# Even attention: another order of scores, transposes, copies and exponentials, and the head sums behind the first projection pair

## The chip, the core and the metric

One Trainium2 chip, one of its cores. The metric is the device time of one execution of the whole kernel in microseconds; the median of several runs counts. The engines are TensorE (PE; its weight loads are listed as PEld), VectorE (DVE), ScalarE (ACT), GpSimd (POOL) and SyncE (SP), which issues most transfers.

## The reference, cut to what matters

The kernel computes two blocks of two layers each on 512 tokens of 1024 features (and 256 context tokens). The change concerns the attention of the first layer of the first block. It has 8 heads with two maps each of width 32; the two softmaxes are subtracted with a factor `lam`, applied to values of width 64, and each head is normalised afterwards. Queries are 512 tokens that look at 768 keys (context and tokens), and 256 context queries that look at the context alone.

```python
def diff_attend(q, k, v, lam):
    s = jnp.einsum('bqhmd,bkhmd->bhmqk', q, k).astype(jnp.float32) * (A_QK ** -0.5)
    p = jax.nn.softmax(s, axis=-1)
    a = p[:, :, 0] - lam * p[:, :, 1]
    return jnp.einsum('bhqk,bkhd->bqhd', a, v.astype(jnp.float32))

def diff_attention_post(o, subln, lam_init):
    B, N = o.shape[:2]
    return (rms_norm(o, subln) * (1.0 - lam_init)).reshape(B, N, BRANCH_W)
```

Its output, gated, is multiplied with `w_out[0]` (1024 x 1024), normalised and added to the stream. Before this stage come modulation, input norm and input projection, and after it the odd layer and the second block; all of these are unchanged.

## The kernel before, in words

All five engines run one program each and meet through semaphores. Each engine works strictly in the order in which its program is written.

The even attention runs over 48 units `EVEN_UNITS` = (hp, t, a): head pair hp (4), query tile t of 128 rows (6), head a of the pair (2). Tiles t < 4 are token queries with 768 keys (large units), tiles 4 and 5 context queries with 256 keys (small units). Units 12 to 15, for instance, are the first large ones of the second head pair.

- `even_scores(u)` on TensorE (L556) makes both maps of unit u, in three terms (high times high, high times low, low times high), into banks 0 to 2 or 3 to 5. It waits until the exponentials of unit u-2 have read these banks (`ea["exp"]`).
- VectorE takes the maximum (`even_max`, L1613). ScalarE makes the two exponentials (`even_exp`, L1074), one for each map, with row sums. VectorE divides and mixes the two maps (L1627, L1628, L1631), which signals `probs`. It runs over the units in order: mix u, then maximum of u+2, and at some units other work: low parts of the next head pair (`even_lo`, L1567, behind (t, a) = (2, 0)), the gate of the previous one (`gated_head`, L1616), the split of `eob` (L1422, L1423, behind (4, 1)), and at u = 20 and 37 the split of a weight panel of the output projection (`split_at`, L1403 and L1404).
- `even_transposes(u, kts, n)` (L482) transposes the mixed probabilities, key tiles 0 to 3 into bank 6 and then 4 and 5 into the same bank; between them ScalarE must have copied the bank (`even_copy`, L941, into `ept`; semaphores `transposed` and `copied`, counted by `moved`). Small units have only key tiles 4 and 5.
- `even_pv(p, half)` (L587) multiplies the copies of a pair of units (both heads of one tile) with the values, half of the key tiles at a time, into bank 7. `even_out` on ScalarE copies bank 7 out.
- ScalarE in a step u: both exponentials of u+1, then both copies of u, then at some units `even_hi` (high parts of the next head pair), `even_out` and `even_square`.

On TensorE a step u is: scores of u+2, wait for `probs` of u, transposes 0 to 3 of u, one half of the values of an earlier pair, transposes 4 and 5 of u.

Behind the attention come `head_sums(t)` (L622: sums of squares of each head, two columns a product), the output projection in eight steps `out0_pair(i)` (L329 to L331, L385 to L387), the first two with parts of the other branch that are ready early, and `head_spread(t)` (L632). VectorE makes variances from the four head sums, ScalarE the root, VectorE the inverse. SyncE loads weight panels 1 and 2 of this projection once the scores of units 23 and 47 are done.

Of the kernel before, what the change touches and what calls it, by code (L numbers as in the profile page):

```python
# [28 lines left out]
ACT = mybir.ActivationFunctionType  # L29
# [5 lines left out]
P = 128  # L35
D = 1024
KT = D // P
TX, TC = 512, 256
TA = TX + TC
# [49 lines left out]
def build_kernel(nc, dram, out):  # L89
    with ExitStack() as ctx:  # L90
# [42 lines left out]
        stat = sb("stat", [P, 96])  # L133
# [190 lines left out]
        def _(pe):  # L324
# [194 lines left out]
            for e in range(2, 16):  # L519
# [7 lines left out]
                if e in MOD1_AFTER:  # L527
                    m = MOD1_AFTER.index(e)
# [74 lines left out]
            even_scores(1)  # L603
            mod_columns(1, 11)
            pe.wait_ge(mod_ready, 6)
            for u, (hp, t, a) in enumerate(EVEN_UNITS):
                if u + 2 < len(EVEN_UNITS):
                    even_scores(u + 2)
                pe.wait_ge(ea["probs"], u + 1)
                if t < 4:  # L610
                    even_transposes(u, range(4), moved[u])
                if u >= 2:
                    even_pv(u // 2 - 1, u % 2)
                even_transposes(u, range(4, 6), moved[u] + (t < 4))
            even_pv(len(EVEN_UNITS) // 2 - 1, 0)
            even_pv(len(EVEN_UNITS) // 2 - 1, 1)

            def head_sums(t):

# [31 lines left out]
                    if i == KT - 1:  # L651
                        last.then_inc(panel_done, 1)

            for t in range(3):
                head_sums(t)
            out0_pair(0)
            head_sums(3)
            out0_pair(1)
            pe.wait_ge(ea["out"], 8)
            for t in range(4):  # L660
# [66 lines left out]
            n = 0  # L727
# [197 lines left out]
        def _(act):  # L925
# [14 lines left out]
            def copy(o, in_, func=ACT.Identity, **kw):  # L940
                return act.activation(o, in_, func, **kw)  # L941
# [120 lines left out]
            act.wait_ge(ea["lam"], 1)  # L1062
            tell(copy(lam4[:, 0:2], lam4[:, 0:2], ACT.Exp), ea["lam_exp"], 1)

            def even_exp(u):
                t, b = EVEN_UNITS[u][1], 3 * (u % 2)
                act.wait_ge(ea["negmax"], u + 1)
                if u >= 3:
                    act.wait_ge(ea["transposed"], moved[u - 2])
                flat = ps[:, b:b + 3, :].rearrange("p b n -> p (b n)")  # L1070
                for m in range(2):
                    n = TA if t < 4 else TC
                    at = m * (TA if t < 4 else 512)
                    act.activation(prob[u % 3][:, m, 0:n], flat[:, at:at + n], ACT.Exp,  # L1074
                                   bias=stat[:, 2 * (u % 4) + m:2 * (u % 4) + m + 1],
                                   accum_out=stat[:, 8 + u % 4:9 + u % 4] if m else stat[:, 32 + u:33 + u])\
                        .then_inc(ea["exp"], 1)

            def even_copy(u):
                if u >= 4:  # L1080
                    act.wait_ge(ea["pv"], u // 2 - 1)
                for i, kts in enumerate(((0, 4), (4, 6))[2 - EVEN_MOVES[u]:]):
                    act.wait_ge(ea["transposed"], moved[u] + i + 1)
                    copy(ept[u % 4][:, kts[0]:kts[1], :], ps[:, 6, 0:(kts[1] - kts[0]) * P]
                         .rearrange("p (k n) -> p k n", n=P)).then_inc(ea["copied"], 1)

            def even_square(hp):
                copy(esq[:, hp, :], eot[:, hp, :], ACT.Square).then_inc(ea["sq"], 1)
# [3 lines left out]
                cols = (slice(0, TX), slice(TX, TA))[part]  # L1092
                tell(copy(eot[:, hp, cols], ps[:, 7, 0:(TX, TC)[part]]), ea["out"], 2 * hp + part + 1)

            even_exp(0)
            for u, (hp, t, a) in enumerate(EVEN_UNITS):
                if u + 1 < len(EVEN_UNITS):
                    even_exp(u + 1)
                even_copy(u)
                if (t, a) == (1, 0) and hp < 3:  # L1100
                    even_hi(hp + 1)
                if (t, a) == (0, 1) and hp:
                    even_out(hp - 1, 1)
                    even_square(hp - 1)
                elif (t, a) == (4, 1):
                    even_out(hp, 0)
            act.preload_act_table(ACT.Sqrt)
            even_out(3, 1)
            even_square(3)
# [273 lines left out]
        def _(dve):  # L1383
# [239 lines left out]
            for u, (hp, t, a) in enumerate(EVEN_UNITS):  # L1623
                n = TA if t < 4 else TC
                i = u % 4
                dve.wait_ge(ea["exp"], 2 * u + 2)
                step(dve.reciprocal(stat[:, 12 + i:13 + i], stat[:, 8 + i:9 + i]))  # L1627
                step(dve.scalar_tensor_tensor(out=stat[:, 16 + i:17 + i], in0=stat[:, 32 + u:33 + u], scalar=lam4[:, 3:4],  # L1628
                                              in1=stat[:, 12 + i:13 + i], op0=ALU.mult, op1=ALU.mult))
                p = prob[u % 3]  # L1630
                dve.scalar_tensor_tensor(out=p[:, 0, 0:n], in0=p[:, 1, 0:n], scalar=stat[:, 16 + i:17 + i],  # L1631
                                         in1=p[:, 0, 0:n], op0=ALU.mult, op1=ALU.add).then_inc(ea["probs"], 1)
                if u + 2 < len(EVEN_UNITS):
                    even_max(u + 2)
                if (t, a) == (2, 0) and hp < 3:
                    even_lo(hp + 1)
                if (t, a) == (2, 1) and hp:
                    dve.wait_ge(ea["out"], 2 * hp)
                    gated_head(hp - 1)
                if (t, a) == (4, 1):  # L1640
                    split_tensor(h1hi, h1lo, np.s_[:, 4 + hp, :], eob[:, hp, :], ea["mixed"], hp + 1)
                if u in (20, 37):
                    split_at(FIRST["out0"] + (u == 37))
# [450 lines left out]
```

## Time and profile before

| | us |
|---|---|
| median of 3 runs | 2546.95 |
| lowest and highest run | 2537.63, 2559.36 |
| the profiled execution | 2544.75 |
| its span | 2543.0 |
| TensorE busy in the span | 2344.8 (92%) |
| VectorE busy | 1411.4 (56%) |
| ScalarE busy | 588.8 (23%) |

The profile comes from one execution. Times in it count from the start of the span. A row of instructions gives line, engine and operation, output and inputs, the count, busy time and mean duration, and the idle time of the engine before them with what released it. Matmuls overlap in the pipeline, so the distance from start to start tells more than a matmul's own duration. PEclk is the clock granted to TensorE as a share of 2.4 GHz.

### The profile page before, as it was taken

To read this page: it belongs to the slowest core of one execution; us is meant where nothing else is said; L and a number is where in the kernel's file an instruction comes from. 1 tells how busy PE (TensorE), PEld (TensorE's weight loads), DVE (VectorE), ACT (ScalarE), POOL (GpSimd) and SP (SyncE) were. 2 spreads that over 40 slices of the span, in tenths; PEclk is the share of its full clock that TensorE was granted. 3 is DMA by queue.
4 is the path that set the end of the run, shared out by engine and by line. 5 is a ranking of instruction groups with operands and counts; after the bars stand their busy time and mean duration, and the time that the engine had idled before them with its cause. 6 is when DMAs were issued, how large, how long until landed. Compare 5 with 4: busy or idle time off the path is not lost.

```text
span 2543.0 us, 28907 instructions
## 1 busy us (share of the span) xinstructions
PE 2344.8 (92%) x12276; PEld 1918.4 (75%) x12276; DVE 1411.4 (56%) x1673; ACT 588.8 (23%) x1138; POOL 88.1 (3%) x57
## 2 busy tenths in 40 slices
PE   6999898999999978987799999999999999999997
PEld 5787786667878744675478888879988787888886
DVE  2232336774463068564957776354478734787633
ACT  2111005552230246125622111011110001211100
POOL 0000000000000122021100000000000000000000
PEclk9899997568899999997899999999999999999998
DMA  8022120000121201110012232222222122232222
GB/s 335 18 100 99 71 112 34 18 1 17 67 83 51 84 24 48 59 67 17 34 67 83 100 100 79 93 94 83 87 80 83 67 99 100 83 100 93 85 92 79
DMA packets 30704, 196.03 MB, mean 77 GB/s; under 512 B 3440, under 2 KB 3696, under 8 KB 12528
## 3 DMA queue, kind: packets, MB, share of 16 engines
q1 hardware_dynamic: 29136, 188.03, 21.0%
q10 hardware_dynamic: 1440, 6.16, 0.7%
q8 instruction: 97, 1.59, 0.3%
q14 instruction: 31, 0.25, 0.0%
HBM read 192.08 MB, written 2.10 MB: 76 GB/s over the span
## 4 chain that ended last, share of the span: by engine, by line
PE 85%; DVE 11%; ACT 2%; issue 1%; POOL 1%; DMA 1%; SPq 0%; DVEq 0%; ACTq 0%; POOLq 0%
PE ps L329 20%; PE ps L330 20%; PE ps L331 20%; PE ps L385 3%; PE ps L386 3%; PE ps L387 3%; PE ps L482 3%; PE ps L556 2%; PE ps L438 2%; PE ps L587 1%; PE ps L764 1%; PE ps L741 1%; PE ps L422 1%; PE ps L917 1%; PE ps L463 1%
## 5 line engine op out<-in xcount | busy, mean ns | idle before, releaser
L1403 DVE CAST whi<-raw 128x2048 fp32r<-128x2048 f32 (+2 forms) x162 | 183.8, 1135 | 484.8 <-DMA raw<-in_ffn_out 117.5
L329 PE MATMUL ps<-h2hi,whi 128*128 128x512 f32 x1040 | 409.3, 394 | 18.3 <-DVE h2lo L1500 12.2
L330 PE MATMUL ps<-h2lo,whi 128*128 128x512 f32 x1040 | 406.9, 391 | 0.0
L331 PE MATMUL ps<-h2hi,wlo 128*128 128x512 f32 x1040 | 406.6, 391 | 0.0
L1404 DVE TENSOR_TENSOR wlo<-raw,whi 128x2048 fp32r<-128x2048 f32 (+2 forms) x162 | 341.6, 2109 | 5.6
L329 PE MATMUL ps<-h1hi,whi 128*128 128x512 f32 (+1 forms) x768 | 276.4, 360 | 16.4 <-DVE h1lo L1445 8.3
L330 PE MATMUL ps<-h1lo,whi 128*128 128x512 f32 (+1 forms) x768 | 271.4, 353 | 0.0
L331 PE MATMUL ps<-h1hi,wlo 128*128 128x512 f32 (+1 forms) x768 | 269.1, 350 | 0.0
L329 PEld LDWEIGHTS ps<-h2hi,whi 128*128 128x128 f32 x1040 | 196.7, 189 | 60.9 <-issue 13.8
L331 PEld LDWEIGHTS ps<-h2hi,wlo 128*128 128x128 f32 x1040 | 196.6, 189 | 41.3
L330 PEld LDWEIGHTS ps<-h2lo,whi 128*128 128x128 f32 x1040 | 196.8, 189 | 40.3
L329 PE MATMUL ps<-mhi,whi 128*128 128x512 f32 x544 | 213.0, 392 | 6.6 <-DVE mlo L1423 3.9
L330 PE MATMUL ps<-mlo,whi 128*128 128x512 f32 x544 | 212.6, 391 | 0.0
L331 PE MATMUL ps<-mhi,wlo 128*128 128x512 f32 x544 | 212.5, 391 | 0.0
L329 PEld LDWEIGHTS ps<-h1hi,whi 128*128 128x128 f32 x768 | 148.9, 194 | 43.6 <-issue 17.7
L330 PEld LDWEIGHTS ps<-h1lo,whi 128*128 128x128 f32 x768 | 148.4, 193 | 20.1 <-issue 1.8
L331 PEld LDWEIGHTS ps<-h1hi,wlo 128*128 128x128 f32 x768 | 147.8, 192 | 20.3
L941 ACT ACTIVATE temp<-ps 128x512 f32<-128x512 f32 (+1 forms) x48 | 25.4, 564 | 439.9 <-PE ps L331 433.8
L385 PE MATMUL ps<-whi,h2hi 128*128 128x256 f32 x416 | 119.8, 288 | 8.0 <-DVE h2lo L1500 4.4
L329 PEld LDWEIGHTS ps<-mhi,whi 128*128 128x128 f32 x544 | 102.8, 189 | 29.2 <-issue 4.3
L386 PE MATMUL ps<-wlo,h2hi 128*128 128x256 f32 x416 | 119.4, 287 | 0.0
L387 PE MATMUL ps<-whi,h2lo 128*128 128x256 f32 x416 | 119.3, 287 | 0.0
(247 smaller groups left out, 3573.5 us busy)
## 6 DMA issues: line engine op xcount, KB each, us to landing
raw<-in_ffn_in SPq DMA_DIRECT2D x44, 1024.0 KB, 4.9
raw<-in_ffn_out SPq DMA_DIRECT2D x32, 704.0 KB, 4.1
raw<-in_even SPq DMA_DIRECT2D x16, 1024.0 KB, 7.0
mod_w<-in_mod SPq DMA_DIRECT2D x6, 2048.0 KB, 25.7
mraw<-in_mod SPq DMA_DIRECT2D x12, 1024.0 KB, 4.9
raw<-in_odd SPq DMA_DIRECT2D x12, 1024.0 KB, 4.9
raw<-in_sgu_v SPq DMA_DIRECT2D x12, 1024.0 KB, 4.8
raw<-in_sgu_u SPq DMA_DIRECT2D x12, 1024.0 KB, 4.8
```

The lines of the kernel that those rows point to most:

```text
L329: pe.matmul(o, r(lhi), r(rhi), start=first, stop=False, **kw)
L330: pe.matmul(o, r(lhi), r(rlo), start=False, stop=False, **kw)
L331: return pe.matmul(o, r(llo), r(rhi), start=False, stop=last, **kw)
L385: pe.matmul(o, lhi, rhi, start=first, stop=False, **kw)
L386: pe.matmul(o, lhi, rlo, start=False, stop=False, **kw)
L387: return pe.matmul(o, llo, rhi, start=False, stop=last, **kw)
L422: last = pe.matmul(mod_bank(layer, k)[32 * g:32 * g + 32, :], cs[:, kt, :], panel[:, kt * 256:(kt + 1) * 256], start=half == 0, stop=half ...
L438: done = pe.matmul(ps[:, 6, 48 + t:49 + t], tile[:, t * P:(t + 1) * P], ones[:, 0:1], start=first and t == tiles[0], stop=last, skip_group ...
L482: return pe.transpose(o, in_, ident)
L556: return pe.matmul(o, r(q), r(k), start=i == 0, stop=i == 2)
L1403: step(dve.tensor_copy(whi[:, slot, 0:width].bitcast(F32R), raw[:, slot, 0:width]))
L1404: tell(dve.tensor_tensor(wlo[:, slot, 0:width].bitcast(F32R), raw[:, slot, 0:width], whi[:, slot, 0:width], ALU.subtract), split_done, n + 1)
```

## The change

On TensorE a step u becomes: scores of u+2, transposes 4 and 5 of u-1, one half of the values of an earlier pair (half a pair later than before), wait for `probs` of u, transposes 0 to 3 of u. On ScalarE a step u becomes: first copy of u-1, first exponential of u+1, second copy of u-1, second exponential of u+1; `even_hi`, `even_out` and `even_square` move one unit later. On VectorE `gated_head` moves one unit later. Transposes still use the transpose mode of TensorE. Behind the attention the first projection pair comes before the four head sums, where it came behind three of them.

```diff
--- before.py
+++ after.py
@@ -603,17 +603,21 @@
             even_scores(1)
             mod_columns(1, 11)
             pe.wait_ge(mod_ready, 6)
+            last_unit = len(EVEN_UNITS) - 1
             for u, (hp, t, a) in enumerate(EVEN_UNITS):
-                if u + 2 < len(EVEN_UNITS):
+                if u < last_unit - 1:
                     even_scores(u + 2)
+                if u:
+                    even_transposes(u - 1, range(4, 6), moved[u] - 1)
+                if u >= 3:
+                    even_pv((u - 3) // 2, (u - 3) % 2)
                 pe.wait_ge(ea["probs"], u + 1)
                 if t < 4:
                     even_transposes(u, range(4), moved[u])
-                if u >= 2:
-                    even_pv(u // 2 - 1, u % 2)
-                even_transposes(u, range(4, 6), moved[u] + (t < 4))
-            even_pv(len(EVEN_UNITS) // 2 - 1, 0)
-            even_pv(len(EVEN_UNITS) // 2 - 1, 1)
+            even_pv((last_unit - 2) // 2, 1)
+            even_transposes(last_unit, range(4, 6), moved[last_unit + 1] - 1)
+            even_pv(last_unit // 2, 0)
+            even_pv(last_unit // 2, 1)
 
             def head_sums(t):
 
@@ -651,10 +655,9 @@
                     if i == KT - 1:
                         last.then_inc(panel_done, 1)
 
-            for t in range(3):
+            out0_pair(0)
+            for t in range(4):
                 head_sums(t)
-            out0_pair(0)
-            head_sums(3)
             out0_pair(1)
             pe.wait_ge(ea["out"], 8)
             for t in range(4):
@@ -1062,27 +1065,27 @@
             act.wait_ge(ea["lam"], 1)
             tell(copy(lam4[:, 0:2], lam4[:, 0:2], ACT.Exp), ea["lam_exp"], 1)
 
-            def even_exp(u):
+            def even_exp(u, m):
                 t, b = EVEN_UNITS[u][1], 3 * (u % 2)
-                act.wait_ge(ea["negmax"], u + 1)
-                if u >= 3:
-                    act.wait_ge(ea["transposed"], moved[u - 2])
+                if m == 0:
+                    act.wait_ge(ea["negmax"], u + 1)
+                    if u >= 3:
+                        act.wait_ge(ea["transposed"], moved[u - 2])
                 flat = ps[:, b:b + 3, :].rearrange("p b n -> p (b n)")
-                for m in range(2):
-                    n = TA if t < 4 else TC
-                    at = m * (TA if t < 4 else 512)
-                    act.activation(prob[u % 3][:, m, 0:n], flat[:, at:at + n], ACT.Exp,
-                                   bias=stat[:, 2 * (u % 4) + m:2 * (u % 4) + m + 1],
-                                   accum_out=stat[:, 8 + u % 4:9 + u % 4] if m else stat[:, 32 + u:33 + u])\
-                        .then_inc(ea["exp"], 1)
-
-            def even_copy(u):
+                n = TA if t < 4 else TC
+                at = m * (TA if t < 4 else 512)
+                act.activation(prob[u % 3][:, m, 0:n], flat[:, at:at + n], ACT.Exp,
+                               bias=stat[:, 2 * (u % 4) + m:2 * (u % 4) + m + 1],
+                               accum_out=stat[:, 8 + u % 4:9 + u % 4] if m else stat[:, 32 + u:33 + u])\
+                    .then_inc(ea["exp"], 1)
+
+            def even_copy(u, late):
+                kts = (range(4), range(4, 6))[late]
+                act.wait_ge(ea["transposed"], moved[u + 1] if late else moved[u] + 1)
                 if u >= 4:
                     act.wait_ge(ea["pv"], u // 2 - 1)
-                for i, kts in enumerate(((0, 4), (4, 6))[2 - EVEN_MOVES[u]:]):
-                    act.wait_ge(ea["transposed"], moved[u] + i + 1)
-                    copy(ept[u % 4][:, kts[0]:kts[1], :], ps[:, 6, 0:(kts[1] - kts[0]) * P]
-                         .rearrange("p (k n) -> p k n", n=P)).then_inc(ea["copied"], 1)
+                copy(ept[u % 4][:, kts[0]:kts[-1] + 1, :], ps[:, 6, 0:len(kts) * P]
+                     .rearrange("p (k n) -> p k n", n=P)).then_inc(ea["copied"], 1)
 
             def even_square(hp):
                 copy(esq[:, hp, :], eot[:, hp, :], ACT.Square).then_inc(ea["sq"], 1)
@@ -1092,18 +1095,26 @@
                 cols = (slice(0, TX), slice(TX, TA))[part]
                 tell(copy(eot[:, hp, cols], ps[:, 7, 0:(TX, TC)[part]]), ea["out"], 2 * hp + part + 1)
 
-            even_exp(0)
+            even_exp(0, 0)
+            even_exp(0, 1)
+            last_unit = len(EVEN_UNITS) - 1
             for u, (hp, t, a) in enumerate(EVEN_UNITS):
-                if u + 1 < len(EVEN_UNITS):
-                    even_exp(u + 1)
-                even_copy(u)
-                if (t, a) == (1, 0) and hp < 3:
+                if u and EVEN_UNITS[u - 1][1] < 4:
+                    even_copy(u - 1, 0)
+                if u < last_unit:
+                    even_exp(u + 1, 0)
+                if u:
+                    even_copy(u - 1, 1)
+                if u < last_unit:
+                    even_exp(u + 1, 1)
+                if (t, a) == (1, 1) and hp < 3:
                     even_hi(hp + 1)
-                if (t, a) == (0, 1) and hp:
+                if (t, a) == (1, 0) and hp:
                     even_out(hp - 1, 1)
                     even_square(hp - 1)
-                elif (t, a) == (4, 1):
+                elif (t, a) == (5, 0):
                     even_out(hp, 0)
+            even_copy(last_unit, 1)
             act.preload_act_table(ACT.Sqrt)
             even_out(3, 1)
             even_square(3)
@@ -1634,7 +1645,7 @@
                     even_max(u + 2)
                 if (t, a) == (2, 0) and hp < 3:
                     even_lo(hp + 1)
-                if (t, a) == (2, 1) and hp:
+                if (t, a) == (3, 0) and hp:
                     dve.wait_ge(ea["out"], 2 * hp)
                     gated_head(hp - 1)
                 if (t, a) == (4, 1):
```

## Rows read from the trace of the kernel before

**Rows 1.** The page, its first line.
```profile
span 2543.0 us, 28907 instructions
```
**Rows 2.** Busy time by stretches: stretch, length, each engine's busy time, PEclk, DMA share, GB/s.
```profile
397.00:427.00 30.00, 28.62 (x155) 21.92 (x151) 20.85 (x27) 16.57 (x36) 0.00 (x0) 0.50 0.01 1
...
509.50:519.70 10.20, 7.59 (x73) 5.82 (x72) 7.42 (x11) 8.88 (x19) 0.00 (x0) 1.00 0.00 0
...
588.00:601.60 13.60, 13.38 (x58) 12.37 (x59) 1.02 (x1) 2.68 (x4) 0.00 (x0) 0.50 0.00 0
...
394.00:589.30 195.30, 174.53 (x1129) 128.36 (x1129) 141.77 (x216) 119.64 (x289) 0.68 (x1) 0.63 0.04 15
```
**Rows 3.** The chain of waits in order of time: start, us, what.
```profile
416.39 2.23 PE ps L556 x10
418.62 1.04 PE ps L482 x4
419.66 1.48 PE ps L587 x12
421.76 2.23 PE ps L556 x10
...
491.40 2.23 PE ps L556 x10
494.87 2.23 PE ps L556 x10
```
**Rows 4.** Timeline of TensorE: start, us, instruction; a unit at 2.4 GHz.
```profile
461.89 0.51 PE L556 MATMUL ps<-wlo,whi 32*128 32x256 f32 x2
...
463.14 0.66 PE L482 MATMUL ps<-mats,prob 128*128 128x128 f32 x4
...
465.06 0.51 PE L556 MATMUL ps<-wlo,whi 32*128 32x256 f32 x2
```
**Rows 5.** Waits of TensorE, 391 to 640 us: us in total, times, longest.
```profile
PE ps L482 <- DVE temp L1631: 6.0, 4, 2.1
PE ps L587 <- DVE prob L1631: 4.9, 3, 2.2
PE ps L482 <- ACT ept L941: 3.5, 4, 1.5
...
PE ps L482 <- DVE prob L1631: 1.9, 2, 1.7
```
**Rows 6.** Timeline of TensorE: three of its waits, in brackets the idle time.
```profile
468.21 0.87 PE L482 MATMUL ps<-mats,temp 128*128 128x128 f32 x4 [1.83 <-DVE temp L1631]
...
485.76 1.55 PE L587 MATMUL ps<-ept,ev 128*64 128x128 f32 x12 [2.19 <-DVE prob L1631]
487.24 0.69 PE L482 MATMUL ps<-mats,prob 128*128 128x128 f32 x2
...
513.82 0.44 PE L482 MATMUL ps<-mats,prob 128*128 128x128 f32 x2 [1.53 <-ACT ept L941]
```
**Rows 7.** Timeline of VectorE around the panel split of unit 37.
```profile
554.83 2.29 DVE L1404 TENSOR_TENSOR wlo<-raw,whi 128x2048 fp32r<-128x2048 f32 x1
557.16 0.16 DVE L1627 RECIPROCAL stat<-stat 128x1 f32<-128x1 f32 x1
...
557.61 1.02 DVE L1631 SCALAR_TENSOR_TENSOR temp<-temp,stat 128x768 f32<-128x768 f32 x1
```
**Rows 8.** Groups by line and shape, 391 to 590 us: busy us, mean ns.
```profile
L1613 DVE TENSOR_REDUCE stat<-ps 128x2 f32<-128x1536 f32 x32 | 56.1, 1756 | 32.5 <-PE ps L556 32.5
...
L1074 ACT ACTIVATE prob<-ps,stat 128x768 f32<-128x768 f32 x48 | 42.6, 896 | 4.9 <-DVE stat L1613 4.3
...
L941 ACT ACTIVATE ept<-ps 128x256 f32<-128x256 f32 x48 | 18.4, 383 | 51.5 <-PE ps L482 51.3
```
**Rows 9.** Timeline of TensorE: the head sums, three heads and then one.
```profile
589.28 7.84 PE L622 MATMUL ps<-mats,esq 128*128 128x2 f32 x36
...
603.39 1.40 PE L622 MATMUL ps<-mats,esq 128*128 128x2 f32 x12
```

## Prediction, made before the changed kernel was run

> **What bounds the kernel now.** I read the page first: one core, a span of 2543.0 us [rows 1]. The change lies only in the even attention and in the head sums behind it, 394 to about 605 us, 8% of the span, so a 1% effect (25 us, about what a measurement of this kernel can tell from no change) needs an eighth of that stage. The busy time by stretches [rows 2] gives two facts. TensorE is busy 174.5 of the 195.3 us of the attention: it is nearly the bound. And its granted clock averages 0.63 there, with only the levels 0.50 (1.2 GHz) and 1.00 (2.4 GHz): from 0.63 = 0.5 + 0.5x, about a quarter of the stage, 51 us, ran at 2.4 GHz. The clock is low although the engine is busy: 28.62 of 30 us between 397 and 427 at 0.50.
>
> The chain of waits [rows 3] gives a unit (one head, one tile of 128 queries; 48 of them) at 1.2 GHz: 2.23 us of scores (L556), 1.04 of the first four transposes (L482), 1.48 of value products (L587), and 421.76 - 421.14 = 0.62 for the last two transposes: 5.37 us, back to back, TensorE alone. A unit whose value products are the four short ones takes 3.47 (491.40 to 494.87), also TensorE alone. At 2.4 GHz [rows 4] the scores take 463.14 - 461.89 = 1.25 and the unit 465.06 - 461.89 = 3.17.
>
> TensorE's waits [rows 5] are 6.0 + 4.9 + 1.9 us for the mixed probabilities of VectorE and 3.5 us for ScalarE's copies, 16.3 in all. Single ones [rows 6]: 1.83 before 468.21 (behind the low parts of queries and keys, L1567, unit 17), 2.19 before 485.76 (behind the weight split of u = 20), 1.53 before 513.82 (copies queued behind `even_hi`). A fourth, 2.13 us at 556.5, is seen from VectorE [rows 7]: the subtraction of a weight panel's split (2.29 us, behind its cast) stands before the reciprocal of 557.16, and the probabilities end at 557.61 + 1.02 = 558.63.
>
> **The change, part by part.** *Nothing is removed.* Every matmul, transpose, copy and exponential stays. Changes between matmul and transpose stay four a unit: before scores, 4 transposes, values, 2 transposes; after scores, 2 transposes of the unit before, values, 4 transposes. So TensorE's own 5.37 us a unit stay. No DMA moves; the weight loads of SP wait for the same score counts.
>
> *What the order hides.* The wait for the probabilities of unit u now stands behind two transposes and the value products: 0.62 + 1.48 = 2.1 us more cover at 1.2 GHz, about 1.2 at 2.4. Of the wait of 2.19 some 0.3 is left (the same VectorE work ends then with the values), of 2.13 some 0.7 (that unit has the short values), of two of 1.8 (unit 17 and its like, 29, at 2.4 GHz) 0.7 each, of the one of 1.7 (unit 42; the last entry of VectorE in [rows 5]) about 1.2. That is 1.9 + 1.4 + 2.2 + 0.5 = 6.0 us back. The copy of the last two transposes has the values as cover only if there are values: units 1 and 2 have none, so transposes meet copy 0.4 + 0.1 + 0.39 later, 0.9 us twice, where units 0 and 1 waited about 0.7 each for the same copy, without values too: 0.3 lost. The 1.53 at 513.82 stays nearly (`even_hi` moves one unit on; the next unit's copies and exponentials are queued behind it): 0.3 back. The tail, probabilities of the last unit to last values, has the same links: 0.
>
> *What the order adds.* ScalarE now runs copy A of u-1, exponential 0 of u+1, copy B of u-1, exponential 1 of u+1. Copy B waits for transposes that TensorE issues behind the scores of u+2, and the scores of u+3 wait for exponential 1. That is a loop: scores, 2 transposes (0.69 to the end of the last at 1.2 GHz, 0.44 at 2.4 [rows 6]), hand-over 0.1, copy B 0.38, exponential 0.90 [rows 8], and some 0.3 for hand-overs. At 1.2 GHz: 2.23 + 0.69 + 0.1 + 0.38 + 0.9 + 0.3 = 4.6, under 5.37: hidden, with 0.8 to spare, and gone if that is used up. But for the unit with large scores and short values, which took 3.47, the loop is 4.6: three such units (11, 23, 35) lose 1.1 each, 3.3 us. At 2.4 GHz: 1.25 + 0.44 + 0.1 + 0.38 + 0.9 + 0.3 = 3.4 against 3.17: 0.2 in some nine large units, 1.8 us. Small units at 2.4 GHz lose up to 0.5 each, eight of them, but VectorE binds there too: between 0 and 4, I take 1. VectorE's own unit is 1.75 for the maximum [rows 8] and 1.47 from reciprocal to probabilities [rows 7], with a gap 3.3: it hides most of the 3.4. Sum of additions: 6.1.
>
> *The head sums.* Before, 36 products of two columns take 7.84 us at 1.2 GHz (0.22 each), the first pair of the projection runs from about 597 to 603.39, and the last 12 take 1.40 at 2.4 GHz (0.12 each) [rows 9]: 589.3 to 604.7. The clock rose at 601.6 [rows 2], 4.6 us into the dense pair. After, the pair goes first: 6.4 us, then 48 sums. At 2.4 GHz these take 5.6, in all 12.0 instead of 15.4: 3.4 back. But 36 of these sums did not raise the clock before; if it falls in the middle of the 48, half of them cost 0.1 more (2.4) and the next pair some 2: 1 lost. Between -3.4 and +1, I take -1. The squares of ScalarE and the wait for `sq` lie under the pair. VectorE's variance chain starts where it did, under the second pair.
>
> *The clock.* It fell back to 1.2 GHz at 468.5 and 519.7, each time behind a stretch with one of the 1.8 us waits (7.59 us busy of 10.2 [rows 2]). With 0.7 instead it may hold for the rest of that group of heads. In the one group VectorE's weight split binds anyway (0), in the other some 15 us instead of 18: half of 3, so -1.5.
>
> **Sum.** -6.0 - 0.3 + 0.3 + 3.3 + 1.8 + 1 - 1 - 1.5 = -2.4. The profiled execution took 2544.75 us (span 2543.0 and 1.75 around it), the median of the runs is 2546.95 (2537.63 to 2559.36). -2.4 gives 2542.4 and 2544.6; I write 2543.
>
> **The rivals.**
> *A. The waits go and nothing comes for them* (18%). For it: they are TensorE's only waits, and the loop is hidden in a usual unit at 1.2 GHz. Against: 3.4 is over 3.17, and 4.6 over 3.47. Then 13 of the 16.3 us go and the sums bring 3: 2529.
> *B. The clock holds at 2.4 GHz* (8%). TensorE idles less, so its clock could stay up. Against: at 397 to 427 it was 95% busy at 0.50. Then VectorE binds: its 141.8 us busy in the stage [rows 2] and 0.2 of gaps in each of 48 units make 151 us for 195: -44, 2501; with half of it 2523. The Trainium skill (TensorE: Matmul & The Clock Gate, section "Why this matters for your kernels") advises to keep TensorE continuously busy, so as to have its full clock. By that rule fewer waits would give this rival's time; the rows of 397 to 427 disagree with it, so it keeps a small chance.
> *C. The exponential behind the copy becomes the bound* (12%), the other side. Place: scores of u+3 waiting for exponential 1. It decides once the loop is over 5.37 at 1.2 GHz, that is when hand-overs and ScalarE's extra work (the outputs, `even_hi`) cost 0.8 more than I put. At 0.5 us beyond, 24 units lose 12 us; and gaps of that kind keep the clock from rising, which costs the 51 us at 2.4 GHz from 13 us (only its busy part, 7.59 of 10.2 us, stretched by 5.37/3.17) to 35 (all of it). 12 + 16 gives 2573; without the clock's part 2557.
> *D. My forecast* (62%): about as many waits come as go. Its own range is 2533 to 2553: the bounds of the head sums (-3.4 to +1), of the small units (0 to 4), and the moments at which the clock rises, where one large unit more or less at 2.4 GHz is 2.2 us.
>
> **The numbers.** The runs of the kernel before lie 22 us apart, so the range for a median goes from A with part of B (2524) to C without its clock part (2560). Faster by over 1% (below 2521): most of B, 0.06. Slower by over 1% (above 2572): half of C, 0.06. Within 1%: 0.88.
>
> **What would show it.** Right: usual units at 1.2 GHz still 5.37 us from scores to scores; the waits behind the weight splits (2.19, 2.13) down to under 0.8; new waits of TensorE's score matmuls (L556) for ScalarE's exponential, about 1 us in units 11, 23 and 35 and some 0.2 at 2.4 GHz; first projection pair directly behind the last values. Wrong: score waits in every unit (C); a granted clock well over 0.63 in the stage (B) or 0.5 throughout; no waits on the exponential at all (A); head sums at 0.22 us each behind the pair.

## The result, and the profile after

| | before | after |
|---|---|---|
| median, us | 2544.45 (8 runs) | 2530.94 (8 runs) |
| lowest and highest | 2537.63, 2559.36 | 2523.49, 2531.98 |
| span of the profiled execution | 2543.0 | 2528.7 |

The ratio is 0.9931 with a 95% interval of 0.991 to 0.9952: 13.5 us less by the medians. The forecast was 2543, a gain of 2.4, with 2524 to 2560 as its range. The time lies in the range and within 1%, but below the 2533 to 2553 that the forecast gave for its own account of the change (rival D), and the size of the gain was missed by a factor of more than five. One run of the kernel before, beside four of the experiments, took 3010.97 us at a granted clock of 0.719 and is left out of every figure below.

Where the 14.3 us between the two spans lie can be read from three stretches. The attention begins with the first scores and ends with the last values; behind it come head sums and two projection pairs, up to the first `head_spread`. First the stretches of the kernel before and then those of the changed one (stretch, length, busy time of PE, PEld, DVE, ACT, POOL, PEclk, DMA share, GB/s):

```profile
391.00:589.30 198.30, 177.10 (x1157) 130.63 (x1157) 143.60 (x218) 119.64 (x289) 1.09 (x1) 0.64 0.06 21
...
589.30:608.90 19.60, 19.60 (x98) 18.18 (x97) 3.65 (x7) 1.64 (x4) 0.00 (x0) 0.69 0.00 0
```

```profile
393.00:575.80 182.80, 166.59 (x1157) 123.45 (x1157) 143.75 (x218) 119.16 (x289) 1.09 (x1) 0.68 0.06 23
...
575.80:594.40 18.60, 18.60 (x98) 17.06 (x97) 3.64 (x7) 2.13 (x4) 0.00 (x0) 0.72 0.00 1
```

The attention is 15.5 us shorter, the sums and pairs 1.0. The stage began 2.0 us later in this execution, and what follows it takes 1934.1 and 1934.3 us; 2.0 - 15.5 - 1.0 + 0.2 gives the 14.3. The same 1157 matmuls are in both rows, so the attention falls into two parts: TensorE's busy time is 10.5 us less (177.10 to 166.59), since more of the same work ran at the higher clock, and its idle time is 5.0 us less (21.2 to 16.2). In this pair of executions the clock is the larger part.

The waits of TensorE in the changed kernel, 396 to 600 us (us in total, times, longest), against [rows 5]:

```profile
PE ps L556 <- ACT prob L1077: 3.8, 8, 1.1
PE ps L556 <- DVE modc L1540: 2.7, 1, 2.7
PE ps L482 <- DVE temp L1642: 2.6, 3, 1.1
PE ps L482 <- DVE prob L1642: 2.3, 4, 0.9
PE ps L556 <- DVE prob L1642: 1.9, 1, 1.9
PE ps L482 <- ACT ept L944: 1.1, 2, 0.6
PE ps L587 <- ACT ept L944: 0.5, 1, 0.5
PE ps L556 <- ACT temp L1077: 0.2, 1, 0.2
```

The smaller entries of the kernel before, which [rows 5] leaves out:

```profile
PE ps L556 <- DVE modc L1529: 2.7, 1, 2.7
...
PE ps L587 <- DVE temp L1631: 0.7, 2, 0.5
PE ps L587 <- ACT ept L941: 0.5, 1, 0.5
```

The waits for mixed probabilities fell from 13.5 us (the 12.8 of [rows 5] and the 0.7) to 2.6 + 2.3 + 1.9 = 6.8, those for ScalarE's copies from 4.0 to 1.6 (the 16.3 us that the prediction counts for both leave out the 0.7 and the 0.5). New are 4.0 us of score matmuls behind an exponential. The wait for `modc` was there before, with the same 2.7.

The chain of waits shows the usual unit at 1.2 GHz (start, us, what). From scores to scores it is 416.02 - 410.65 = 5.37, the length of [rows 3], in the new order: scores, two transposes, values, four transposes.

```profile
410.65 2.23 PE ps L556 x10
413.50 1.48 PE ps L587 x12
414.98 1.05 PE ps L482 x4
416.02 1.29 PE ps L556 x10
```

The last line, 1.29 for the same scores that took 2.23, is at 2.4 GHz already. In the kernel before, the clock rose near 427.6, two units later (in the scores of unit 8, here in those of unit 6). The stretches at the higher clock in the kernel before ([rows 2] has a fourth, 509.50 to 519.70):

```profile
427.60:441.20 13.60, 11.81 (x123) 8.35 (x119) 11.08 (x23) 10.22 (x31) 0.00 (x0) 1.00 0.01 2
...
461.70:468.50 6.80, 4.89 (x47) 3.74 (x46) 5.60 (x8) 4.78 (x11) 0.00 (x0) 1.00 0.00 0
...
567.50:588.00 20.50, 15.98 (x160) 11.18 (x158) 16.06 (x31) 14.86 (x42) 0.00 (x0) 1.00 0.16 53
```

Two of those in the changed kernel, with a stretch at the lower clock between:

```profile
415.90:439.80 23.90, 20.50 (x205) 15.19 (x204) 21.16 (x37) 18.54 (x49) 0.00 (x0) 1.00 0.01 2
439.80:456.90 17.10, 17.10 (x89) 12.46 (x89) 12.81 (x17) 12.05 (x26) 0.00 (x0) 0.50 0.00 1
456.90:477.30 20.40, 16.21 (x164) 11.76 (x164) 18.75 (x28) 13.66 (x38) 0.00 (x0) 1.00 0.16 53
```

The middle row is busy for 17.10 of 17.10 us and stays at 0.50; the third is busy for 16.21 of 20.40 and stays at 1.00. Within the attention TensorE was at 2.4 GHz for 53.7 us before and for 66.8 after; both figures include some 2 us at its very start.

### The profile page after: what moved, and what is told of

The parts are those of the page before. It is cut to its first block, busy times and chain, and to the rows that moved or that the text cites. A ratio compares the mean times of both kernels' runs of the same rounds, so it can differ in the third digit from the quotient of the medians.

```text
span 2528.7 us, 28943 instructions
## 1 busy us (share of the span) xinstructions
PE 2335.9 (92%) x12276; PEld 1911.6 (76%) x12276; DVE 1411.4 (56%) x1673; ACT 589.1 (23%) x1138; POOL 88.3 (3%) x57
## 3 DMA queue, kind: packets, MB, share of 16 engines
q1 hardware_dynamic: 29136, 188.03, 21.1%
## 4 chain that ended last, share of the span: by engine, by line
PE 84%; DVE 11%; ACT 2%; issue 1%; POOL 1%; DMA 1%; SPq 0%; DVEq 0%; ACTq 0%; POOLq 0%
PE ps L329 20%; PE ps L330 20%; PE ps L331 20%; PE ps L385 3%; PE ps L386 3%; PE ps L387 3%; PE ps L482 2%; PE ps L556 2%; PE ps L438 2%; PE ps L767 1%; PE ps L744 1%; PE ps L587 1%; PE ps L422 1%; PE ps L920 1%; PE ps L463 1%
## 5 line engine op out<-in xcount | busy, mean ns | idle before, releaser
L1414 DVE CAST whi<-raw 128x2048 fp32r<-128x2048 f32 (+2 forms) x162 | 183.8, 1135 | 482.2 <-DMA raw<-in_ffn_out 117.4
L331 PEld LDWEIGHTS ps<-mhi,wlo 128*128 128x128 f32 x544 | 102.7, 189 | 21.5
L330 PEld LDWEIGHTS ps<-mlo,whi 128*128 128x128 f32 x544 | 102.8, 189 | 21.2
```

Of the source, the lines that this page charges most:

```text
L330: pe.matmul(o, r(lhi), r(rlo), start=False, stop=False, **kw)
L331: return pe.matmul(o, r(llo), r(rhi), start=False, stop=last, **kw)
L1414: step(dve.tensor_copy(whi[:, slot, 0:width].bitcast(F32R), raw[:, slot, 0:width]))
```

## The experiments

Each kernel ran beside the kernel before on the same chip, whose median there was 2546.58 (e1 to e4), 2547.03 (e6 to e9) or 2545.83 (e5, e10 to e12). The table has the medians, the ratio to the kernel before, and for the profiled execution of each the attention (first scores to last values), the part of it at 2.4 GHz, TensorE's busy and its idle time in it, in us. The names are those of the recorded expectations.

| kernel | median | ratio (95%) | attention | at 2.4 GHz | busy | idle |
|---|---|---|---|---|---|---|
| before | 2544.45 | | 198.3 | 53.7 | 177.1 | 21.2 |
| after | 2530.94 | 0.9931 (0.991, 0.9952) | 182.8 | 66.8 | 166.6 | 16.2 |
| e1_sums_moved | 2545.73 | 0.9986 (0.9967, 1.0006) | 196.5 | 57.1 | 174.6 | 21.9 |
| e2_order_only | 2526.09 | 0.9911 (0.9884, 0.9937) | 182.9 | 66.8 | 166.6 | 16.3 |
| e3_tensor_order | 2562.73 | 1.0058 (1.004, 1.0077) | 219.7 | 53.6 | 180.6 | 39.1 |
| e4_scalar_order | 2534.34 | 0.9949 (0.9928, 0.997) | 195.9 | 57.1 | 173.9 | 22.0 |
| e8_before_late2 | 2539.69 | 0.9983 (0.9966, 1.0001) | 191.4 | 74.1 | 167.1 | 24.3 |
| e7_before_late4 | 2556.66 | 1.002 (0.9996, 1.0044) | 211.7 | 22.9 | 196.0 | 15.7 |
| e9_after_late2 | 2519.49 | 0.99 (0.9886, 0.9915) | 175.8 | 76.9 | 160.4 | 15.4 |
| e6_after_late4 | 2527.12 | 0.9929 (0.9901, 0.9957) | 189.5 | 53.0 | 176.1 | 13.4 |
| e5_exp_first_at_5 | 2520.55 | 0.9899 (0.9879, 0.9919) | 177.8 | 72.0 | 163.2 | 14.6 |
| e10_order_again | 2526.65 | 0.9919 (0.99, 0.9938) | 182.8 | 66.8 | 166.6 | 16.2 |
| e11_after_again | 2532.02 | 0.9939 (0.9919, 0.996) | 183.8 | 64.3 | 168.2 | 15.6 |
| e12_exp_always_first | 2536.24 | 0.9967 (0.9953, 0.9982) | 187.9 | 54.8 | 173.7 | 14.2 |

### The head sums alone

```diff
-            for t in range(3):
-                head_sums(t)
             out0_pair(0)
-            head_sums(3)
+            for t in range(4):
+                head_sums(t)
             out0_pair(1)
```

> Only the head sums move behind the first projection pair; the attention is that of before. Theory W (waits and loop as predicted, sums worth about 1 us): 0 to 2 us faster, the same attention length as before, the pair starting directly behind the last values. Theory K (the gain is mostly made behind the attention): 8 us or more faster. As its attention is that of before, its trace is also a second sample of how long TensorE is at 2.4 GHz there (51 us of 198 in the first).

Measured: 2545.73 against 2546.58 of the kernel before beside it, ratio 0.9986, an interval that holds 1. The stretch from last values to first spread takes 18.8 us (19.6 before). So the move gains about 0.8 us where the attention is that of before, and the gain of the change is not made here. Theory W holds.

### The order of the attention alone

The changed kernel with the diff above taken back.

> The new order of the attention alone; three head sums ahead of the first pair as before. Theory W: 11 to 15 us faster, the rest of the change's 13.5 us. Theory K: 5 us or less. Its trace is a second sample of the new attention: if the clock was chance, the time at 2.4 GHz differs from the 64 us of the changed kernel by 10 us or more; if the order itself holds the clock, it is near 64.

Measured: 2526.09, ratio 0.9911, 20 us faster than the kernel before beside it, more than the 11 to 15 of theory W, and 4.9 less than the changed kernel's median. The attention is that of the changed kernel to 0.1 us, with the same 66.8 us at 2.4 GHz. So the order is all of the gain, and moving the sums takes some of it back. The reason is in the timeline of TensorE. First the kernel with the order alone, its 36 and 12 sums with two products of the pair between them, and its whole stretch up to the spread (second fence, busy times as above); then the changed kernel, which has 48 sums behind the pair.

```profile
573.79 4.28 PE L626 MATMUL ps<-mats,esq 128*128 128x2 f32 x36
577.93 0.77 PE L329 MATMUL ps<-h1hi,whi 128*128 128x512 f32 x1
...
581.58 0.39 PE L329 MATMUL ps<-h1hi,whi 128*128 128x512 f32 x1
...
583.67 1.40 PE L626 MATMUL ps<-mats,esq 128*128 128x2 f32 x12
```

```profile
573.80:589.20 15.40, 15.40 (x98) 14.09 (x97) 3.65 (x7) 2.12 (x4) 0.00 (x0) 0.89 0.00 0
```

```profile
580.10 7.45 PE L626 MATMUL ps<-mats,esq 128*128 128x2 f32 x48
...
587.41 0.77 PE L329 MATMUL ps<-h1hi,whi 128*128 128x512 f32 x1
587.99 0.63 PE L330 MATMUL ps<-h1lo,whi 128*128 128x512 f32 x1
```

The new attention ends at 2.4 GHz. In the old place the 36 sums then take 0.12 us each instead of 0.22 [rows 9]. The clock falls behind them, 0.77 for the first product of the pair, and is back within 3.4 us, so the average clock of the stretch is 0.89. In the new place it falls inside the 48 sums (0.155 each), the second pair starts at 1.2 GHz, 0.77 and 0.63 a product, and the average is 0.72. 18.6 us against 15.4: the move that gains 0.8 us behind the old attention loses 3.2 behind the new one.

Both kernels ran once more, beside each other:

> The new attention with the head sums where they were, again, beside the changed kernel on the same chip. Theory H (the attention now ends at 2.4 GHz, the head sums first run at that clock, the pair behind them keeps it; the move spoils this): 3 to 5 us faster than the changed kernel. Rival: the difference of the first comparison was chance, 0 to 2 us.

> The changed kernel itself, beside the one with the head sums where they were. Theory H: 3 to 5 us slower than that one; attention about 183 us with 67 us of 2.4 GHz if its moments repeat.

2526.65 and 2532.02: 5.4 us apart, after 4.9 the first time. Eleven of the twelve runs with the old place are at or below 2528.05, and twelve of the fourteen with the new one are above 2528.5. So the difference is no chance, and theory H is right in direction, at its upper end or just above it. One link of it is wrong: the pair behind the 36 sums does not keep the clock, it starts at 1.2 GHz (577.93 above) and regains it. Of the gap 3.2 us is in the traces; what the rest is was not shown.

### Half of the order

Only TensorE's new program, with ScalarE's old one (the tail behind the loop, as in the change, is left out here):

```diff
...
+                if u:
+                    even_transposes(u - 1, range(4, 6), moved[u] - 1)
+                if u >= 3:
+                    even_pv((u - 3) // 2, (u - 3) % 2)
                 pe.wait_ge(ea["probs"], u + 1)
                 if t < 4:
                     even_transposes(u, range(4), moved[u])
-                if u >= 2:
-                    even_pv(u // 2 - 1, u % 2)
-                even_transposes(u, range(4, 6), moved[u] + (t < 4))
...
```

> Only TensorE's order is new (last two transposes and values ahead of the wait for the probabilities); ScalarE still makes both exponentials of u+1 and then both copies of u, and waits with its second copy for transposes that now come behind the next scores. Theory W (cover for the probabilities is what pays, ScalarE's order matters little): 8 to 14 us faster. Rival S (both orders are needed, as ScalarE's second copy then holds up the exponentials of the next unit): no gain or slower, score matmuls waiting for exponentials in every unit.

Measured: 2562.73, ratio 1.0058, 16 us slower. My theory W is wrong here and rival S right, though the waits come 27 times in the 48 units and not in every one. The waits (in total, times, longest) and lines of the timeline:

```profile
PE ps L556 <- ACT prob L1078: 21.7, 19, 2.1
PE ps L556 <- ACT temp L1078: 8.7, 8, 1.8
```

```profile
416.04 0.38 ACT L945 ACTIVATE ept<-ps 128x256 f32<-128x256 f32 x1 [2.52 <-PE ps L482]
416.32 0.83 ACT L945 ACTIVATE whi<-eq 128x768 fp32r<-128x768 f32 x1
417.05 0.83 ACT L945 ACTIVATE wlo<-ek 128x768 fp32r<-128x768 f32 x1
...
417.79 0.89 ACT L1078 ACTIVATE prob<-ps,stat 128x768 f32<-128x768 f32 x1
...
418.66 0.90 ACT L1078 ACTIVATE prob<-ps,stat 128x768 f32<-128x768 f32 x1
...
419.70 0.80 PE L556 MATMUL ps<-wlo,whi 32*128 32x256 f32 x2 [1.18 <-ACT prob L1078]
```

ScalarE stood 2.52 us before its second copy, since the transposes for it now come behind the next scores, and both exponentials of the next unit stood behind that copy; the scores after them then waited 1.18. At this unit the two copies of `even_hi` (416.32 and 417.05) stood there too; the scores of the unit before, without them, waited 0.58. There are 30.4 us of such waits in all: the loop that I had priced for the whole change (copy, exponential, scores) with both exponentials in it in place of one. So ScalarE's new order is no refinement. It takes one exponential out of the loop, and without it TensorE's order loses.

Only ScalarE's new program, with TensorE's old one and `gated_head` in its old place (only the lines that set the new order are shown):

```diff
...
+                if u and EVEN_UNITS[u - 1][1] < 4:
+                    even_copy(u - 1, 0)
+                if u < last_unit:
+                    even_exp(u + 1, 0)
+                if u:
+                    even_copy(u - 1, 1)
+                if u < last_unit:
+                    even_exp(u + 1, 1)
...
```

> Only ScalarE's order is new; TensorE keeps 4 transposes, values, 2 transposes of the same unit. Theory W: slower, as the first copy of u now stands behind both exponentials of u+1 and one step later, so that TensorE's last two transposes wait for it: 5 to 25 us slower. Rival: ScalarE's order alone brings the gain: 8 us or more faster.

Measured: 2534.34, ratio 0.9949, 12 us faster than the kernel before beside it; its profiled execution was the slowest of its runs at 2544.78. My theory W failed outright. The rival's number, 8 us or more, came true. I had misread the order: the first copy of u-1 stood right behind the second exponential of u before too, and all that moves is the first exponential of u+1, ahead of the second copy. So almost nothing waits longer (one score wait of 0.4 us for an exponential), and its trace shows idle time as before (22.0 us against 21.2) and nearly the attention of e1 (195.9 against 196.5, both with 57.1 us at 2.4 GHz). The gain of the median lies in other executions, at a higher clock, which the next section weighs; no trace of such a run of this kernel exists, so why its clock is higher stays open.

### Shifting the attention against the clock

Two or four small products of two columns ahead of the third unit's scores, about 0.9 or 1.7 us of extra work with an unused output, in both kernels (four are shown):

```diff
...
             pe.wait_ge(mod_ready, 6)
+            for _ in range(4):
+                pe.matmul(ps[:, 7, 0:2], ident, blk[:, 0:P:64], start=True, stop=True)
...
```

> The kernel before with two fillers, about 0.9 us, another place against the clock's moments. Theory P: differs from the four fillers and from none by several us in either direction. Theory O: 0 to 2 us slower than before, 50 to 60 us at 2.4 GHz.

> The kernel before with the same four fillers, about 1.7 us. Theory P: its time at 2.4 GHz in the attention moves by 10 us or more from 53.7 in one direction. Theory O: it stays at 50 to 60 and the kernel is 1 to 3 us slower than before.

> The changed kernel with two fillers, about 0.9 us. Theory P: its time at 2.4 GHz differs from 66.8 us by 10 us or more in this or in the run with four fillers, towards the 54 of before. Theory O: 60 to 72 us, and the kernel 0 to 2 us slower than the changed kernel.

> The changed kernel with four small filler products (two columns each, output not used) on TensorE ahead of the third score unit: the attention is shifted by about 1.7 us against the moments at which the clock can change. Theory P (the higher clock of the changed kernel is where its blocks fall on these moments): its time at 2.4 GHz in the attention moves by 10 us or more from 66.8, and its attention from 182.8 by 5 us or more beyond the 1.7. Theory O (the order itself keeps the clock up): 60 to 72 us at 2.4 GHz, attention 183 to 187.

The attention stretches of the kernel before with two and with four fillers, then of the changed kernel with two and with four:

```profile
386.30:577.70 191.40, 167.08 (x1161) 123.44 (x1161) 143.28 (x218) 119.60 (x289) 1.09 (x1) 0.69 0.06 22
```

```profile
391.40:603.10 211.70, 196.01 (x1165) 145.11 (x1165) 143.57 (x218) 119.97 (x289) 1.09 (x1) 0.55 0.05 20
```

```profile
386.00:561.80 175.80, 160.38 (x1160) 119.55 (x1160) 142.75 (x218) 118.58 (x289) 1.09 (x1) 0.72 0.07 24
```

```profile
392.30:581.80 189.50, 176.09 (x1165) 131.44 (x1165) 144.26 (x218) 119.04 (x289) 1.09 (x1) 0.64 0.06 22
```

With about one microsecond of useless work the old attention was 6.9 us shorter in its profiled execution, with two 13.4 us longer: its time at 2.4 GHz went from 53.7 to 74.1 and to 22.9. The changed kernel went from 66.8 to 76.9 and to 53.0. These are single executions, and the kernel before without any filler has runs 21 us apart, at clocks of 0.919 to 0.934, so the traces alone do not show that the fillers did it. The medians of all runs go the same way in three cases: 2539.69 and 2556.66 against the 2547.03 beside them (both intervals of the ratio still hold 1), and 2519.49 for the changed kernel with two, whose four runs all have a higher clock (0.939 to 0.942) than any of the fourteen runs of the changed kernel (0.934 to 0.937). In the fourth case they do not: the changed kernel with four has a median of 2527.12, below the 2530.94 without fillers, though its profiled execution (2535.8) has the longer attention. So theory P is right in that a shift of a microsecond can move the clock, shown for the changed kernel with two fillers (it ran beside another group than the changed kernel itself, but the kernel before has medians within 1.2 us of each other in all groups) and likely for the old one. Theory O has a part too: at each of the three shifts the new order had more of the higher clock (13.1, 2.8 and 30.1 us more) and less idle time (5.0, 8.9 and 2.3 us less), and its attention is shorter by 15.5, 15.6 and 22.2 us. Three pairs of executions do not settle whether the order itself keeps the clock up.

Idle time can't be compared without the clock either. In the old order it was 15.7, 21.2 and 24.3 us where 22.9, 53.7 and 74.1 us ran at 2.4 GHz: at the higher clock TensorE gets ahead of the others more often. Read between these three, and for the last value just beyond them, the old order would idle for about 21.1, 23.2 and 24.7 us at the new order's 53.0, 66.8 and 76.9 us; the new one idled for 13.4, 16.2 and 15.4. By this estimate it saves 7 to 9 us of waits, not the 5.0 of the first pair.

The runs without a trace can be read in the same way. Each run has a mean granted clock for the whole program. Over 66 runs of the kernel before, at clocks of 0.919 to 0.934, a straight line through time against clock has 2545.5 us at 0.93 and falls by 1.43 us for each 0.001. The line follows nine tenths of the spread (the squared correlation is 0.91). Against it, extended up to 0.9405, and each at its own clock:

| kernel | mean clock of its runs | mean us | from the line |
|---|---|---|---|
| before | 0.9281 | 2548.1 | 0 |
| e1_sums_moved | 0.9292 | 2546.3 | -0.2 |
| after (8 runs) | 0.9351 | 2529.9 | -8.3 |
| e11_after_again | 0.9348 | 2531.7 | -6.8 |
| e2_order_only | 0.9363 | 2525.8 | -10.6 |
| e10_order_again | 0.9365 | 2526.4 | -9.8 |
| e4_scalar_order | 0.9349 | 2536.0 | -2.5 |
| e3_tensor_order | 0.9298 | 2562.4 | +16.6 |
| e8_before_late2, e7_before_late4 | 0.9326, 0.9246 | 2541.3, 2553.8 | -0.5, +0.6 |
| e9_after_late2, e6_after_late4 | 0.9405, 0.9360 | 2519.7, 2528.7 | -10.7, -8.1 |
| e5_exp_first_at_5 | 0.9390 | 2521.4 | -11.2 |
| e12_exp_always_first | 0.9302 | 2538.3 | -6.8 |

At an equal clock the new attention is worth 7 to 11 us, which agrees with the 7 to 9 estimated from the idle times, and its runs have a clock that is higher by 0.007, worth another 10. (Together that is the 18 us between the two means; the medians of the result are 13.5 apart.) The fillers leave the first number alone and move the second. The 16.6 of the half order are waits. Of the gain of ScalarE's order alone only 2.5 are not clock: its mean clock, 0.9349, is as high as the changed kernel's 0.9351, although its one trace has the long waits of the kernel before, up to 3.4 us. So these runs do not show that the shorter waits are what raised the clock.

### The exponential behind the copy

In the order without the moved sums, the second exponential goes ahead of the second copy at the three units with large scores and short values:

```diff
...
+                first = (t, a) == (5, 1) and hp < 3
+                if first:
+                    even_exp(u + 1, 1)
                 if u:
                     even_copy(u - 1, 1)
-                if u < last_unit:
+                if u < last_unit and not first:
                     even_exp(u + 1, 1)
...
```

> The new order of the attention with three head sums ahead of the first pair, and at the three units u = 11, 23 and 35 ScalarE makes the second exponential of u+1 ahead of the second copy of u-1. Theory L (the loop scores, transposes, copy, exponential, scores costs 0.9 us at each of these units): these waits of score matmuls (1.1 us longest) go and the attention is 2 to 3 us shorter than the 182.9 of the same kernel without this, if the clock stays; the moments of the clock may shift it either way by several us. Rival: another wait takes their place and the attention is as long as before this edit.

The wait in the changed kernel that this is about, unit 11, and the attention of the kernel with the edit:

```profile
438.55 0.51 PE L556 MATMUL ps<-wlo,whi 32*128 32x256 f32 x2 [1.12 <-ACT prob L1077]
```

```profile
392.30:570.10 177.80, 163.20 (x1156) 121.43 (x1156) 143.08 (x218) 118.80 (x289) 1.09 (x1) 0.70 0.07 23
```

The median is 2520.55, ratio 0.9899 (0.9879 to 0.9919), the best kernel of this study without fillers and 10 us under the changed one. Its idle time is 1.7 us less than that of the same kernel without the edit, its busy time 3.4 us less, which is clock. At unit 23, at 1.2 GHz, the wait is gone: the scores follow after 3.47 us, as before the change, where the changed kernel took 4.36. At unit 11, at the higher clock, 0.85 of the 1.12 stays:

```profile
441.50 0.51 PE L556 MATMUL ps<-wlo,whi 32*128 32x256 f32 x2 [0.85 <-ACT prob L1078]
```

At unit 35, now at the higher clock too, it is 0.84 where it was 0.82. So about 1.1 us of the 2.8 at the three units went, less than the 2 to 3 of theory L, and 0.75 of the 1.7 us of idle time is the wait for `modc`, ahead of all three. The runs say the same: at an equal clock this kernel is about 1 us better than the one without the edit (11.2 below the line against 10.6 and 9.8). The rest of its gain of 5.8 us is clock.

In every unit:

```diff
...
-                if u:
-                    even_copy(u - 1, 1)
                 if u < last_unit:
                     even_exp(u + 1, 1)
+                if u:
+                    even_copy(u - 1, 1)
...
```

> The new order with three head sums ahead of the first pair, and ScalarE makes both exponentials of u+1 between the two copies of u-1 in every unit. Theory L: no score matmul waits for an exponential any more, but transposes 0 to 3 of u wait for the later second copy at 2.4 GHz (0.3 to 0.6 us a unit), while at 1.2 GHz nothing is lost: within 5 us of the same kernel without this. Rival C (the exponential behind the copy binds everywhere): 10 us or more faster.

Measured: 2536.24, 10 us slower than the order alone. Rival C is out: the exponential does not bind everywhere. Theory L named the mechanism and missed the size, as transposes waited for copies

```profile
PE ps L482 <- ACT ept L945: 6.2, 10, 1.4
```

for 6.2 us and yet the idle time of the whole attention fell (14.2 against 16.3). That is no gain of the edit: only 54.8 us ran at 2.4 GHz, and the new order with 53.0 us there, the one with four fillers, idled for 13.4. At an equal clock this kernel is 3 to 4 us worse than the order alone (6.8 below the line against 10.6 and 9.8); the rest of the 10 us is clock.

## Why the prediction was right or wrong

The time fell into the range because the range reached down to rival A and half of B, not because my account of the change was right. Of its signs, the usual unit of 5.37 us, the waits of about 1 us at units 11, 23 and 35 and the pair directly behind the last values came. The waits behind the weight splits did not go under 0.8 (1.89 and 1.07), and a sign of being wrong came, a granted clock over 0.63 (0.68).

**TensorE's own work.** Right: 5.37 us a usual unit in both orders, the same count of matmuls, the same changes of mode.

**What the order hides.** Right in place and nearly in size. I expected 6.0 us of the waits for probabilities back; 13.5 became 6.8, 6.7 back. The waits behind the low parts of queries and keys were 1.83 and 1.81 (units 17 and 29) and are 0.75 and 0.76 (units 5 and 17, the ones that ran at 2.4 GHz now; 0.7 predicted), and that behind the panel of unit 37 went from 2.13 to 1.07 (0.7 predicted). The one behind the split of unit 20 was forecast at 0.3 from its place at 1.2 GHz and stayed at 1.89, since this unit now ran at 2.4 GHz, where VectorE binds:

```profile
475.54 0.51 PE L556 MATMUL ps<-wlo,whi 32*128 32x256 f32 x2 [1.89 <-DVE prob L1642]
```

The copies I put at no gain: 4.0 became 1.6. The 1.53 behind `even_hi` did not come again, as that unit now ran at 1.2 GHz, where the copy has time.

**What the order adds.** Mis-sized by a third: 6.1 us expected, 4.0 measured (3.8 and 0.2). The three units with large scores and short values lost 1.12, 0.9 and 0.9 (1.1 each predicted). The 1 us put for small units came (five waits of 0.21 or 0.22 us). The 1.8 us for large units at 2.4 GHz did not: the first one took 3.06 us from scores to scores (415.95 to 419.01), less than my loop of 3.4 and less than the 3.17 of [rows 4]. The loop's hand-overs cost less than the 0.4 that I gave them, or the exponential was begun earlier; which, I did not separate. In sum the waits gave 5.0 us back where my terms for them add up to 0.1 lost.

**The head sums.** The 1.0 us of the profiled pair is the 1.0 predicted, and the clock did fall inside the 48 sums, for which I had forecast 1 us lost. So this number was right by luck, and for the wrong neighbour. I priced the move behind an attention that ends at 1.2 GHz; the new one ends at 2.4, and there the old place is better by 3.2 us.

**The clock.** This is the step that failed. I gave it 1.5 us, from two falls behind waits of 1.8 us, and it was 10.5 in the profiled pair. The mechanism that I named can be followed in part: the kernel before left the higher clock at 468.5 and 519.7, right behind those waits, and with two fillers it did so three times, after 6.8 us each; the changed kernel waited 0.75 and 0.76 behind the same work, at units 5 and 17, and kept it for 23.9 and 20.4 us. But these stretches too ended just behind waits, of 1.12 us (before 438.55) and 1.89 us (before 475.54), and the length of a wait does not decide it: in the kernel before the clock fell at 441.2 behind waits of 0.72 and 0.45, and it stayed up at 576.01 behind one of 1.71. What I left out is that the clock also rose earlier, and that it changes from run to run and with small shifts. I had named this as one large unit more or less, 2.2 us; in the traces it was 10 to 31 us of stage time at the other level. What raised the clock of the new order is not shown.

**The rivals.** A (2529, only waits go) comes nearest in time, and for less than half of its reason in the profiled pair: the waits gave 5.0 of the 13 it asked for (7 to 11 by the runs at an equal clock), the sums 1.0 of its 3. B was given 8%: its full form is out (66.8 of 182.8 us at 2.4 GHz), its half form (2523) was nearer than my forecast. The Trainium skill (TensorE: Matmul & The Clock Gate, section "Why this matters for your kernels") ties the full clock to a TensorE that is kept busy without idle gaps. For gaps the rows agree in part: behind 1.83 us the clock fell and behind 0.76 it stayed, but behind 1.71 it stayed too, and behind 0.72 and 0.45 it fell. For being kept busy they do not: 17.10 of 17.10 us busy at 0.50, and the busiest attention of all, 196.01 of 211.70 us, had the lowest clock, 0.55. C is out by e12 and by the 5.37 that stayed.

What a busy stretch must contain for the clock to rise was not tested by itself and stays open.

## What to carry to other kernels

When an in-order engine waits for a result and has other work that is ready, put that work ahead of the wait, but follow the loop through the other engines too: the same order on one engine alone was 16 us slower here, and it paid only once ScalarE's queue was cut to match. Where a stage runs at a mixture of two clocks, split a change's effect into busy time (clock) and idle time (waits) before judging it, compare idle times only where about as much of the stage ran at the higher clock, take many runs of both kernels and not one trace of each, and price a moved step behind the stage as it will be, not as it is.

## What the runs showed of the hardware that I had not expected

- With a microsecond of useless work ahead of the stage the changed kernel was faster: a median of 2519.49 us against 2530.94, with the clock of every run above that of every run without it, and an attention of 175.8 us against 182.8 in the traces. With twice the work the attention of its trace was 6.7 us longer, but the median 3.8 us lower.
- The runs of the kernel before spread over 20 us, and their mean granted clock goes with nine tenths of it: 1.43 us for each 0.001, with 1.7 us left as scatter.
- Products of two columns take 0.22 us each at 1.2 GHz and 0.12 at 2.4: they cost little more than half at the higher clock although they stream almost nothing (7.84 us for 36 in the kernel before, 4.28 in the one with the order alone).
